# Block products over sums for three gate slabs of a feed-forward stage

## What is computed

```python
def _swiglu(h, w_gu, w_down):
    gate, up = jnp.split(h @ w_gu, 2, axis=-1)
    return (jax.nn.silu(gate) * up) @ w_down

def first_block(x, ...):
    x = x + 0.5 * _swiglu(_rmsnorm(x, ffn1_norm[l]), ffn1_w_gu[l], ffn1_w_down[l])
    x = x + _token_mixing(_rmsnorm(x, mix_norm[l]), w_in[l], ...)
    x = x + 0.5 * _swiglu(_rmsnorm(x, ffn2_norm[l]), ffn2_w_gu[l], ffn2_w_down[l])
```

## Time and profile before

| | us |
|---|---|
| median of three runs | 3025.74 (3023.76 to 3028.38) |
| span of the profiled execution | 3022.0 |
| TensorE busy in it | 3001.6 |
| VectorE busy | 1983.5 |
| ScalarE busy | 1449.2 |
| GpSimd busy | 1326.5 |

### The profile page before, as it was taken

The page is one execution under the profiler, slowest core; times in us unless marked ns, Lnnn a source line. Parts: engine busy times, 40 slices in busy tenths (PEclk is TensorE's granted clock), DMA queues, the critical chain, the costliest instruction groups (busy, mean ns, idle before and its releaser), DMA issues.

```text
span 3022.0 us, 46302 instructions
## 1 busy us (share of the span) xinstructions
PE 3001.6 (99%) x18688; PEld 2660.7 (88%) x18688; DVE 1983.5 (66%) x2918; ACT 1449.2 (48%) x1885; POOL 1326.5 (44%) x653
## 2 busy tenths in 40 slices
PE   9999999999999999999999999999999999999998
PEld 7888888888999999998888888888899998999997
DVE  4777665664324457777566666577579866789764
ACT  6444444444657455544544444444544454544454
POOL 5455545445565555585554555444550004710013
PEclk9999999999999999999999999999999999999999
DMA  7888887886776555566688888788576546665555
GB/s 241 274 279 264 273 282 252 290 287 182 226 175 175 158 165 150 151 170 199 214 274 285 268 272 268 263 291 279 172 216 195 161 143 213 183 192 182 154 181 181
DMA packets 491662, 663.33 MB, mean 220 GB/s; under 512 B 70440, under 2 KB 278040, under 8 KB 490936
## 3 DMA queue, kind: packets, MB, share of 16 engines
q1 hardware_dynamic: 485960, 655.85, 68.5%
q0 software_dynamic: 4448, 2.94, 0.3%
q10 hardware_dynamic: 1040, 1.58, 0.2%
HBM read 656.06 MB, written 2.11 MB: 218 GB/s over the span
## 4 chain that ended last, share of the span: by engine, by line
PE 96%; DVE 3%; ACT 0%; issue 0%; POOL 0%; DMA 0%; DVEq 0%; ACTq 0%
PE ps L1088 37%; PE ps L952 20%; PE ps L1093 18%; PE ps L958 10%; PE ps L969 3%; PE ps L974 1%; PE ps L936 1%; DVE narrow_split_slabs L2132 1%; PE ps L1571 1%; PE ps L1350 1%; PE ps L1331 1%; DVE h_split L2089 1%; PE ps L1059 0%; DVE U L2082 0%; PE ps L1358 0%; PE ps L1388 0%
## 5 line engine op out<-in xcount | busy, mean ns | idle before, releaser
L880 POOL TENSOR_TENSOR split_slabs<-stage,split_slabs 128x1024 fp32r<-128x1024 f32 x318 | 775.4, 2439 | 1289.3 <-ACT split_slabs L1627 1289.2
L1627 ACT ACTIVATE split_slabs<-stage 128x1024 fp32r<-128x1024 f32 x592 | 627.3, 1061 | 858.7 <-PE ps L1093 790.8
L1088 PE MATMUL ps<-split_slabs,h_split 128*128 128x512 f32 x3288 | 813.1, 389 | 0.0
L1627 ACT ACTIVATE narrow_split_slabs<-stage 128x1024 fp32r<-128x1024 f32 (+1 forms) x437 | 457.7, 1051 | 611.0 <-PE ps L958 460.6
L1088 PEld LDWEIGHTS ps<-split_slabs,h_split 128*128 128x128 f32 x3288 | 616.9, 188 | 127.9
L2132 DVE TENSOR_TENSOR split_slabs<-stage,split_slabs 128x1024 fp32r<-128x1024 f32 x274 | 354.0, 1292 | 493.0 <-ACT split_slabs L1627 491.1
L952 PE MATMUL ps<-h_split,narrow_split_slabs 128*128 128x256 f32 x4928 | 620.6, 279 | 2.9 <-issue 1.9
L952 PEld LDWEIGHTS ps<-h_split,narrow_split_slabs 128*128 128x128 f32 x4928 | 586.0, 188 | 14.5 <-issue 8.7
L880 POOL TENSOR_TENSOR narrow_split_slabs<-stage,narrow_split_slabs 128x1024 fp32r<-128x1024 f32 (+1 forms) x182 | 441.2, 2434 | 317.5 <-ACT narrow_split_slabs L1627 317.1
L1093 PE MATMUL ps<-split_slabs,h_split 128*128 128x512 f32 x1644 | 439.4, 389 | 0.0
L2132 DVE TENSOR_TENSOR narrow_split_slabs<-stage,narrow_split_slabs 128x1024 fp32r<-128x1024 f32 x255 | 339.5, 1335 | 126.8 <-ACT narrow_split_slabs L1627 125.7
(11 more groups left out here) (309 smaller groups left out, 2516.9 us busy)
## 6 DMA issues: line engine op xcount, KB each, us to landing
stage<-in_ffn_w_gu SPq DMA_DIRECT2D x352, 512.0 KB, 4.9
stage<-in_w_in SPq DMA_DIRECT2D x349, 512.0 KB, 3.9
U<-in_w_ada SPq DMA_DIRECT2D x192, 512.0 KB, 5.4
stage<-in_ffn_w_down SPq DMA_DIRECT2D x176, 512.0 KB, 5.1
stage<-in_w_out SPq DMA_DIRECT2D x96, 512.0 KB, 4.2
stage<-in_w_in SPq DMA_DIRECT2D x80, 128.0 KB, 2.8
stage<-in_w_branch_c SPq DMA_DIRECT2D x32, 192.0 KB, 3.5
stage<-in_cmp_w SPq DMA_DIRECT2D x8, 512.0 KB, 4.9
```

The costliest lines, as they stand in the source:

```text
L880: nc.gpsimd.tensor_tensor(slab_part(n, 1, size(n)), stage[:, n % RING, 0:size(n)], slab_part(n, 0, size(n)).bitcast(F32), ALU.subtract).th ...
L1088: mm(ps[:, 2 * pair + T, :], stationary(kk, i)[:, T * P:(T + 1) * P], w[0][:, kk, :], start=first and kk == 0 and i == 0, stop=False)
L1627: return fn(slab_part(n, 0, size(n)), stage[:, n % RING, 0:size(n)], ACT.Copy)
```

## The change

In groups 1 to 8 of both stages, gate slabs q = 3, 5 and 7 are multiplied another way. With the two chunks kk and the two halves T as a 2 x 2 block matrix of tokens, and two chunks by two halves of 256 columns as a 2 x 2 block matrix of weights, seven block products over sums of blocks give what eight products of blocks give. `summed_passes` issues seven products in three passes, 21 matmuls of 256 columns, in place of 12 of 512.

- The sums of token blocks are made once a stage, in group 0 (`combine`, `round_combined`, `rest_combined`).
- The sums of weight blocks are made for each such slab by VectorE: `sum_slab`, three operations that write into the up pair of banks, which is empty from `gated` until slab 8. ScalarE rounds them out of PSUM, VectorE makes their low part (`rest_sums`). The three plain blocks (768 columns) are rounded by ScalarE and their low part is made by GpSimd (`rest_plain`).
- The partial products of sums lie in banks 4 and 5 as well. After slab 7, ScalarE copies a block (`copy_gate`, q = 11), VectorE adds them up (`sum_gate`, q = 12), and ScalarE takes Silu at q = 14 (`silu_summed`) in place of q = 11.
- Since banks 4 and 5 are taken, the modulation's sums move to bank 6, and the activations are turned in two halves through bank 7 alone, at q = 4, 6, 8 and 9, with 32 transposes of half the size; the second half waits until the first one's low part is made. ScalarE rounds the halves at q = 8 and 11, VectorE makes the low parts at q = 8 and 12.
- In these groups VectorE makes low parts of slabs 10 and 15 and of the sums only; GpSimd makes the others.

The core of the diff:

```diff
+STR_SLABS, STR_GROUPS = (3, 5, 7), range(1, 9)
+STR_COLS = WN // 2
+BY_VECTOR = (10, 15)
+TURN_ACT = {4: (0, 0), 6: (0, 1), 8: (1, 0), 9: (1, 1)}
+ROUND_ACT, REST_ACT = (8, 11), (8, 12)
...
+        summed = [s + 16 * j + q for s in (S_F1, S_F2) for j in STR_GROUPS for q in STR_SLABS]
+        nth_sum = {n: k + 1 for k, n in enumerate(summed)}
+        by_vector -= {s + 16 * j + q for s in (S_F1, S_F2) for j in STR_GROUPS for q in range(16) if q not in BY_VECTOR}
+        by_vector |= set(summed)
...
+            if n in nth_sum:
+                return plain_lo, nth_sum[n]
             return (slab_done, n + 1) if n in plain else slab_split(n)
...
+            def rest_plain(n):
+                pool.wait_ge(plain_hi, nth_sum[n])
+                pool.wait_ge(slab_summed, nth_sum[n])
+                nc.gpsimd.tensor_tensor(plain_part(n, 1), stage[:, n % RING, STR_COLS:SLAB],
+                                        plain_part(n, 0).bitcast(F32), ALU.subtract).then_inc(plain_lo, 1)
...
+            def summed_passes(pair, n, q, first, last):
+                low, high = slice(0, STR_COLS), slice(STR_COLS, WN)
+                of_plain = ((tokens(0, 0), ps[:, 4, low]), (combined(3), ps[:, 2 * pair, low]), (tokens(1, 0), ps[:, 2 * pair, high]))
+                of_sums = ((combined(0), ps[:, 5, low]), (combined(1), ps[:, 5, high]), (combined(2), ps[:, 4, high]),
+                           (tokens(1, 1), ps[:, 2 * pair + 1, high]))
+                pe.wait_ge(plain_hi, nth_sum[n])
+                for k, (stationary, sums_to) in enumerate(of_plain):
+                    for i in range(2):
+                        mm(sums_to, stationary(i), whole[0][:, k, :], start=first and k == 0 and i == 0, stop=False)
+                pe.wait_ge(hi_done, nth[n])
+                for k, (stationary, sums_to) in enumerate(of_sums):
+                    for i in range(2):
+                        mm(sums_to, stationary(i), sums[0][:, k, :], start=first and k == 0 and i == 0, stop=False)
+                pe.wait_ge(plain_lo, nth_sum[n])
+                for k, (stationary, sums_to) in enumerate(of_plain):
+                    mm(sums_to, stationary(0), whole[1][:, k, :], start=False, stop=last and k == 2)
+                pe.wait_ge(*slab_split(n))
+                for k, (stationary, sums_to) in enumerate(of_sums):
+                    ins = mm(sums_to, stationary(0), sums[1][:, k, :], start=False, stop=last and k > 0)
+                ins.then_inc(slab_done, 1)
...
+                    if m in nth_sum:
+                        k = nth_sum[m]
+                        act.wait_ge(*slab_loaded(m))
+                        if k > 2:
+                            act.wait_ge(slab_done, summed[k - 3] + 1)
+                        fn(plain_part(m, 0), stage[:, m % RING, STR_COLS:SLAB], ACT.Copy).then_inc(plain_hi, 1)
+                        act.wait_ge(slab_done, before[m] + 1)
+                        act.wait_ge(slab_summed, k)
+                        fn(slab_part(m, 0), sums_of(m), ACT.Copy).then_inc(hi_done, 1)
+                    elif m not in plain:
...
+            def copy_gate(f, j, s0):
+                act.wait_ge(slab_done, s0 + 16 * j + 8)
+                act.wait_ge(act_turned, 2 * (GU_GROUPS * f + j))
...
+            def silu_summed(f, j, r):
+                act.wait_ge(gate_summed, len(STR_GROUPS) * f + j - STR_GROUPS[0] + 1)
...
+            def round_act(f, j, k):
+                act.wait_ge(act_turned, 2 * (GU_GROUPS * f + j) + k + 1)
+                fn(ats[:, 0, (4 * j + 2 * k) * S:(4 * j + 2 * k + 2) * S], ps[:, 7, :], ACT.Copy).then_inc(act_hi, 1)
...
-                        if j > 0 and q == 10:
-                            round_act(f, j - 1)
+                        if j > 0 and q in ROUND_ACT:
+                            round_act(f, j - 1, ROUND_ACT.index(q))
...
-                        if q == 11:
+                        if j not in STR_GROUPS and q == 11:
                             silu(f, j, s0, r)
+                        if j == 0 and q == 12:
+                            round_combined(f)
+                        if j in STR_GROUPS and q == 11:
+                            copy_gate(f, j, s0)
+                        if j in STR_GROUPS and q == 14:
+                            silu_summed(f, j, r)
...
-                w, total = u(ADA_RING, P, 2, WK, WN)[:, m % 2], ps[:, 5, :]
+                w, total = u(ADA_RING, P, 2, WK, WN)[:, m % 2], ps[:, 6, :]
...
+                def turn_act(j, k, half):
+                    if (k, half) == (0, 0):
                         dve.wait_ge(evacuated, g0 + j + 1)
-                    for b in range(P // SQUARE):
-                        turned_rows = slice(b * SQUARE, (b + 1) * SQUARE)
-                        last = v.transpose(dst[turned_rows, :, :, rows], src[rows, :, :, turned_rows])
-                    if a == P // SQUARE - 1:
+                    if (k, half) == (1, 0):
+                        dve.wait_ge(act_lo, 2 * (GU_GROUPS * f + j) + 1)
+                    for a in (2 * half, 2 * half + 1):
...
+                        for b in range(P // SQUARE):
+                            turned_rows = slice(b * SQUARE, (b + 1) * SQUARE)
+                            last = v.transpose(dst[turned_rows, :, :, rows], src[rows, :, :, turned_rows])
+                    if half:
                         last.then_inc(act_turned, 1)
+                def rest_act(j, k):
+                    at, part = GU_GROUPS * f + j, slice((4 * j + 2 * k) * S, (4 * j + 2 * k + 2) * S)
+                    dve.wait_ge(act_hi, 2 * at + k + 1)
+                    last = v.tensor_tensor(ats[:, 1, part], ps[:, 7, :], ats[:, 0, part].bitcast(F32), ALU.subtract)
                     last.then_inc(act_lo, 1)
+                def turns(j, i):
+                    if i in REST_ACT:
+                        rest_act(j, REST_ACT.index(i))
+                    if i in TURN_ACT:
+                        turn_act(j, *TURN_ACT[i])
+                def sum_slab(n):
+                    j, q = divmod(n - s0, 16)
+                    dve.wait_ge(*slab_loaded(n))
+                    if q == STR_SLABS[0]:
+                        dve.wait_ge(evacuated, g0 + j)
+                    else:
+                        dve.wait_ge(*slab_split(n - q + STR_SLABS[STR_SLABS.index(q) - 1]))
+                    whole, sums = col_blocks(stage[:, n % RING, :]), col_blocks(sums_of(n))
+                    chained(v.tensor_tensor(sums[:, 0:2, :], whole[:, 0:1, :].broadcast_to([P, 2, STR_COLS]), whole[:, 1:3, :], ALU.subtract), "sum1", n)
+                    chained(v.tensor_tensor(sums[:, 2, :], whole[:, 2, :], sums[:, 0, :], ALU.subtract), "sum2", n)
+                    v.tensor_tensor(sums[:, 3, :], whole[:, 3, :], sums[:, 2, :], ALU.subtract).then_inc(slab_summed, 1)
+                def rest_sums(n):
+                    dve.wait_ge(hi_done, nth[n])
+                    v.tensor_tensor(slab_part(n, 1), sums_of(n), slab_part(n, 0).bitcast(F32), ALU.subtract).then_inc(lo_vec, 1)
...
+                def sum_gate(j):
+                    dve.wait_ge(gate_copied, len(STR_GROUPS) * f + j - STR_GROUPS[0] + 1)
+                    part, pair = u(SILU, P, 4, STR_COLS), 2 * gate_acc(f)
+                    fifth = col_blocks(ps[:, 5, :])
+                    chained(v.tensor_tensor(part[:, 2, :], part[:, 1, :], ps[:, 4, STR_COLS:WN], ALU.add), "gate2", f, j)
+                    chained(v.tensor_tensor(part[:, 0:4:3, :], part[:, 2:3, :].broadcast_to([P, 2, STR_COLS]), fifth, ALU.add), "gate3", f, j)
+                    chained(v.tensor_tensor(part[:, 2, :], part[:, 3, :], fifth[:, 0, :], ALU.add), "gate4", f, j)
+                    v.tensor_tensor(u(SILU, P, TT, WN), u(SILU, P, TT, WN), ps[:, pair:pair + 2, :], ALU.add).then_inc(gate_summed, 1)
                 def between(i):
-                    if f == 0 or i not in (1, 3):
+                    if s0 + i - 1 in nth_sum:
+                        rest_sums(s0 + i - 1)
+                    if s0 + i in nth_sum:
+                        sum_slab(s0 + i)
+                    elif f == 0 or i not in (1, 3):
                         slab_lo(s0 + i)
                     for m in range(ADA_LOADS):
                         if ADA_AT[m] == i:
...
                         between(16 * j + q)
-                        if j > 0 and 4 <= q < 8:
-                            turn_act(j - 1, q - 4)
-                        if j > 0 and q == 11:
-                            rest_act(j - 1)
+                        if j > 0:
+                            turns(j - 1, q)
+                        if j in STR_GROUPS and q == 12:
+                            sum_gate(j)
+                        if j == 0 and q == 11:
+                            combine()
```

98 lines of the change are left out of this document (72 added, 26 removed).

## The result

| | before | after |
|---|---|---|
| median of the runs, us | 3025.43 | 3081.47 (3079.29 to 3086.31) |
| span of the profiled execution | 3022.0 | 3077.5 |
| up to the first matmul of the mixing stage | 732.6 | 763.8 |
| second feed-forward stage | 719.4 | 742.5 |
| all the rest of the span | 1570.1 | 1571.2 |

The changed kernel is slower: ratio 1.0185, 95% interval 1.0173 to 1.0198, 56 us. The forecast was 3058, in the right direction, but 24 us short and 1.5 us outside its range. The table splits the 55.5 us of span by the start of the first matmul of each stage: 31.2 us lie in the first feed-forward stage, 23.1 in the second, 1.1 elsewhere.

A forecast was written before the change was run, and what follows sets the result against it. TensorE, busy 99% of the span, was taken as the bound, with VectorE then falling behind. 3022.0 - 11.5 saved + 44 of waits = 3054.5 us of span, plus 3.7 to the median: 3058 us, range 3014 to 3080.

The forecast's parts named there:

- The pieces' prices: Costs of VectorE's added and removed work, together +8.1 us a group: 38.1 busy of 42.8 us, 42.1 with waits.
- the timetable: One group worked through from its first slab on TensorE; the next gated starts 3.6 us late.
- the margin of 0.5 us at slab 10: VectorE's low part of slab 10 ends at 27.75 us; TensorE wants it at 28.3; lateness beyond the margin makes TensorE wait.
- contention: Rival: VectorE and GpSimd collide over SBUF; 3074 us, up to 3100; chance 0.10 for everything over 3078, no saving included.
- the 44 us of waits: TensorE's waits for a late VectorE: 26 us in the first feed-forward stage, 18 in the second.
- The rival's own case of one meeting of 1 us a group: Each group pays one VectorE and GpSimd collision of 1 us more: 16 us, 3074 us in all.
- Its price for the latter, 2.9 us: First stage, five groups: a 2.39 us operation on logit_b and two small ones stand ahead of gated.
- a load takes 4.2 us from the end of the step that frees it; I use 4.4: Two-place ring of modulation loads: this delay holds back steps at places 0 and 2, and so the next gated.
- The timetable's lateness of groups 2 to 8 in the second stage: gated's delay passed on by groups 1 to 7: 3.6, 4.0, 0.6, 4.3, 0, 5.1, 2.6 us; waits 18 us.
- The case of 6 us a load among the bounds: Modulation loads that take 6 us cost six groups 1.6 us more: 3068 us.
- The slab's saving: TensorE, 48 gate slabs: 21 narrow matmuls take 2.48 us, saving 0.24 us a slab, 11.5 us in all.
- The list of what would show it: Profile signs: summed slabs every 2.48 us, VectorE busy some 38 us a group, TensorE idle at slabs 10 and 7.

The follow-up runs named there:

- ten: Changed kernel with slab 10's low part made by VectorE instead of GpSimd in groups 1 to 8; 3098.05 us, ratio 1.0240 to the kernel before.
- poolthin: Changed kernel with GpSimd's low parts cut to 64 columns in groups 2 to 8; 3061.74 us, ratio 1.0121 to the kernel before.

## Why the prediction was right and wrong

**What held.** The direction, the mechanism and the engine: VectorE can't keep to its fixed order, TensorE waits, and the waits exceed the saving. The pieces' prices were good: transposes 0.324 us (0.33), sum_slab 1.62 with its gaps (1.56), the wait inside a slab 1.15 (1.13), sum_gate 2.84 (2.85), the median 4.0 us above the span (3.7). Group 1 was on time and group 2 late, the first stage was worse than the second, and beyond the two stages nothing moved by more than 1.1 us.

**A misreading of the change.** The description of the change and the timetable say that VectorE makes the low part of slab 10. It doesn't. The set `by_vector` holds only odd slabs, and the change takes away all but 10 and 15 from it, so that 15 alone is left: the second stage's groups show one L2244 each, and GpSimd makes 12 whole low parts a group. So the margin of 0.5 us at slab 10, on which the waits were hung, belongs to a kernel that didn't exist; "ten" is that kernel, and it is 17 us slower still: for it the forecast of 3058 is 40 us short. What counts in the changed kernel is a place that the timetable passed by: slab 7's sums, rounded at 17.3 in the timetable and 16.2 us after gated's end in the trace, against TensorE wanting them at 19.4. That leaves 1.6 us by the trace (2.1 by the timetable), and a lateness beyond it is paid in full and a little more: in the second stage 3.9 late gave 3.0 us, 5.5 gave 4.1, 5.4 gave 3.9, 4.2 gave 2.9 and 6.0 gave 4.5. The other two are groups 4 and 6, where sum_slab met GpSimd behind gated: 3.3 late gave 3.6, and 1.9 gave 4.6.

**The step that failed: contention, put at nothing in the sum.** The prediction had it as a rival, with "In my timetable at most one meets GpSimd", and added none of it to the 44 us of waits. poolthin prices it at 15.7 us by the traces (20 by the medians), 7.7 in the second stage and 8.0 in the first, of 62.9 us in all. What is left in poolthin is 47.2 us of waits, 19.7 in the second stage and 27.5 in the first, where the prediction had 18 and 26. So contention is the larger part of the 23 us that the span was short. The rival's own case of one meeting of 1 us a group gave 16 us, the size that was measured, by another path: a few groups with meetings of 1.5 to 2.5 us. The timetable looked for meetings among five operations a group. The meetings that the trace shows ahead of the waits are those of sum_slab's first operation in two groups of the second stage, and in the first stage those of log_sigmoid's small operations, which it didn't count. Its price for the latter, 2.9 us, came from the row of 273.95 in the earlier trace rows, which is a meeting itself: 2.39 us for an operation that takes 0.18 us in poolthin. That row is in group 6 only. The other four groups have four to six other operations each, and not the three that the description names; the five of group 2 took 1.2 us before (98.67 to 99.90) and 5.3 after (100.73 to 106.07).

**A second step was wrong, and another error hid it: "a load takes 4.2 us from the end of the step that frees it; I use 4.4".** One row was taken for a rule. In the group shown above the two loads ahead of gated took 5.6 and 6.2 us. The page's list has the median from issue to landing, both kernels alike:

```profile
U<-in_w_ada SPq DMA_DIRECT2D x192, 512.0 KB, 5.4
```

Weight loads ran beside the load of the earlier trace rows as well. From the landings in the traces, 1.8 other loads were under way beside it on the mean, 2.6 and 2.7 beside the two slow ones. No run varied this alone, so that the number of loads is the reason is not shown.

The timetable's lateness of groups 2 to 8 in the second stage (3.6, 4.0, 0.6, 4.3, 0, 5.1, 2.6) sums to 20.2 us, the trace's (3.9, 5.5, 3.3, 4.2, 1.9, 5.4, 6.0) to 30.2. It was right where it expected much, and wrong in the three groups that it let off. But it took off a margin of 0.5 us a group (slab 10) where the real one is 1.6 (slab 7). The two errors nearly cancel: 18 us forecast for the second stage, 19.7 measured without contention. That the forecast came this near is luck. The case of 6 us a load among the bounds gave 3068, which is closer by number, though not by its reason.

**One more term.** The slab's saving is 0.18 us, not 0.24: a summed slab lasts 2.52 us (2.48 expected from the earlier trace rows), and the slab after it 2.74 instead of 2.72: 8.6 us, not 11.5.

**The sum again.** Saved 8.6 instead of 11.5; waits with what follows from them 27.4 in the second stage instead of 18 (23.1 longer and 4.3 saved) and 35.5 in the first instead of 26: 62.9 instead of 44. 3022.0 - 8.6 + 62.9 + 1.1 = 3077.4. Of the 23 us that the forecast of 3054.5 lacks, 15.7 are contention, 3.2 other waits, 2.9 the saving and 1.1 the rest of the span.

**The list of what would show it.** "TensorE's idle time named by VectorE's low parts, at slab 10 and, where gated is over 2 us late, at slab 7 already": wrong in the name (ScalarE's rounding, which waits for VectorE's sums) and for slab 10, right for slab 7. VectorE's busy time: 36.5 us a group on the mean of groups 2 to 8 of the second stage, not 38.1, and 1.2 of the difference is slab 10's part. Idle for modulation loads at places 0 and 2: right.

What stays open: the parts don't add up to one split. By the medians filling the wait is worth 33 us, the steps' work 27, GpSimd's contention 20, the steps' places 14, log_sigmoid's place 10, and the sums' work all 65; by the traces they are 27, 22, 16, 15, 5 and 62. Each lowers the same lateness until the margin is reached, which would explain that their sum is too large; how they share it was not measured.

## What to carry to other kernels

Where a second engine works through an order written by hand, compare its period in a repeated piece with that of the engine that sets the end, and look for waits inside the piece that its other work could fill. Moving eight transposes into each 1.15 us wait was worth 33 us. List the margins at every hand-over and not at the one that looks tightest, and check in the order of the program, not in the names of a table, which engine does a step. Before an overlap with another engine is put at nothing, look at the short operations of the order too: a row that is far too long for its size may be a meeting already. A load ring's delay is to be taken from the median or the slow rows. Packing its loads densely elsewhere gave new waits here; spreading them evenly did not.

## What was not expected of the hardware

- Operations of 128x32, 0.19 us long, took 2.17 and 2.33 us when they met GpSimd's of 2.4 us: with small operations the loss is up to the other's whole length, not a share of one's own.
- After a wait of 2.86 us TensorE's granted clock dropped. The window from 207 to 213 us has 0.84 on the mean, the next 7 us 0.90, so part of the time was spent at 1.2 and not 2.4 GHz:

```profile
210.44 1.18 PE L1163 MATMUL ps<-split_slabs,combined_split 128*128 128x256 f32 x6 [2.86 <-ACT split_slabs L1722]
...
213.34 2.53 PE L1130 MATMUL ps<-split_slabs,h_split 128*128 128x512 f32 x8
```

  From 210.44 to the next slab took 2.90 us (1.89 after the wait at 1618.40), and that slab 3.30 (2.75), 1.6 us on top of the wait. After the wait of 2.67 us in group 7 the clock was 0.61 on the mean from 353.57 to 358 us; around the one of 2.34 us in group 3 (158 to 168 us) it was 1.00. The waits of 1.0 to 1.3 us, three to a group, were followed by no slower matmuls.
- Two loads of 512 KB were there 5.6 and 6.2 us after the step that freed their place, with 2.6 and 2.7 other loads under way, against 4.2 us with 1.8 others in the earlier trace rows.
